# Norms after residual additions taken by pairs of blocks, the root read from PSUM, and the first feed-forward weights split in the mixer

## What is computed

```python
h = rmsnorm(x, norm1_w[l]) * (1.0 + sc1) + sh1      # shifts, scales and gates: silu(c) @ ada_w[l]
x = x + g1 * hybrid_mixer(h, ...)                   # projections, linear attention, SSD, w_out
h = rmsnorm(x, norm2_w[l]) * (1.0 + sc2) + sh2
ff = swiglu(h, ...) if l == 0 else moe_swiglu(h, ...)  # 1024 -> 3584 -> 1024; 8 experts, top 2
x = x + g2 * ff
```

## Time and profile before

| | |
|---|---|
| median of 3 runs | 2882.19 us (2881.25 to 2882.37) |
| profiled execution, its own time | 2881.89 us |
| its span | 2879.9 us, 35798 instructions |
| PE busy | 2536.7 us (88%) |
| DVE busy | 2091.9 us (73%) |
| ACT busy | 1210.8 us (42%) |
| POOL busy | 256.5 us (9%) |
| DMA | 824.78 MB, mean 286 GB/s |

### The profile page before, as it was taken

One profiled execution on the slowest core, in us unless ns is written; L12 is line 12 of the kernel. 1 busy time (PEld: TensorE's weight loads), 2 busy tenths in 40 slices (PEclk: granted clock), 3 DMA queues, 4 the chain that ended last, 5 costly groups with the idle time before them and its releaser, 6 DMA issues. The chain is left out here.

```text
span 2879.9 us, 35798 instructions
## 1 busy us (share of the span) xinstructions
PE 2536.7 (88%) x14026; PEld 2176.6 (76%) x14026; DVE 2091.9 (73%) x2916; ACT 1210.8 (42%) x1310; POOL 256.5 (9%) x280
## 2 busy tenths in 40 slices
PE   4979997986999999999999967997786898887877
PEld 2869996775888888888888855655675888777877
DVE  5758984754988989899899953537736677777764
ACT  2214432214777777777777742103312222222221
POOL 0000000000000000000000000000001334334331
PEclk8988999996999999999999988998998999999899
DMA  7545874443999999999999925211554999999996
GB/s 324 210 171 203 323 278 162 175 187 121 356 356 356 356 357 357 341 351 357 355 356 357 358 93 210 88 58 54 197 218 174 385 403 416 420 421 420 420 421 286
DMA packets 107469, 824.78 MB, mean 286 GB/s; under 512 B 11736, under 2 KB 13912, under 8 KB 14816
## 3 DMA queue, kind: packets, MB, share of 16 engines
q1 hardware_dynamic: 69568, 550.99, 50.1%
q0 software_dynamic: 36864, 268.45, 22.7%
q10 hardware_dynamic: 864, 3.00, 0.3%
HBM read 821.34 MB, written 1.05 MB: 286 GB/s over the span
## 5 line engine op out<-in xcount | busy, mean ns | idle before, releaser
L1537 DVE TENSOR_TENSOR ring_r<-ring,arena_r 128x2048 fp32r<-128x2048 f32 x336 | 770.1, 2292 | 12.2 <-ACT arena_r L1832 0.8
L1832 ACT ACTIVATE arena_r<-ring 128x2048 fp32r<-128x2048 f32 x378 | 725.5, 1919 | 30.9 <-DMA ring<-in_ffn_w_down 14.4
L605 PE MATMUL ps<-arena_r 128*128 128x512 f32 (+1 forms) x1120 | 417.2, 373 | 1.5 <-DVE arena_r L1542 1.5
L607 PE MATMUL ps<-arena_r 128*128 128x512 f32 x896 | 349.3, 390 | 0.0
L606 PE MATMUL ps<-ring_r,arena_r 128*128 128x512 f32 x896 | 348.6, 389 | 0.0
L1181 PE MATMUL ps<-sel,arena 128*128 128x128 f32 x1904 | 252.2, 297 | 76.9 <-ACT sel L1832 76.9
L591 PE MATMUL ps<-h,ring 128*128 128x256 f32 (+2 forms) x1216 | 277.0, 389 | 41.1 <-ACT h L1832 41.1
L1181 PEld LDWEIGHTS ps<-sel,arena 128*128 128x128 f32 x1904 | 245.0, 212 | 84.0 <-ACT sel L1832 83.8
L1181 PE MATMUL ps<-sel,ring 128*128 128x128 f32 x2192 | 265.5, 283 | 37.7 <-ACT sel L1832 37.7
L591 PEld LDWEIGHTS ps<-h,ring 128*128 128x128 f32 (+2 forms) x1216 | 228.1, 189 | 91.7 <-issue 48.0
L1181 PEld LDWEIGHTS ps<-sel,ring 128*128 128x128 f32 x2192 | 259.4, 198 | 42.7 <-ACT sel L1832 42.2
(11 more groups left out here) (244 smaller groups left out, 3614.1 us busy)
## 6 DMA issues: line engine op xcount, KB each, us to landing
ring<-in_moe_w_gate SPq DMA_DIRECT2D x112, 1024.0 KB, 5.7
ring<-in_moe_w_up SPq DMA_DIRECT2D x112, 1024.0 KB, 6.0
ring<-in_moe_w_down SPq DMA_DIRECT2D x112, 1024.0 KB, 5.4
ring<-in_ada_w SPq DMA_DIRECT2D x16, 2048.0 KB, 8.5
ring<-in_w_in SPq DMA_DIRECT2D x10, 2048.0 KB, 10.6
ring<-in_ada_w SPq DMA_DIRECT2D x16, 1024.0 KB, 9.2
ring<-in_w_ada SPq DMA_DIRECT2D x8, 2048.0 KB, 8.1
ring<-in_ffn_w_gate SPq DMA_DIRECT2D x14, 1024.0 KB, 7.1
```

What stands on the lines that cost most here:

```text
L605: e.matmul(out, xs[0], ws[0], start=start, stop=False, skip_group_check=True)
L607: return e.matmul(out, xs[1], ws[0], start=False, stop=stop, skip_group_check=True)
L1537: v(e.tensor_tensor(ring_low[ring.half[unit]], ring.buf[unit], m.high[unit_at[unit] % NHIGH].bitcast(F32), ALU.subtract), ("low", unit))
L1832: A.mark(e.activation(out, src, func, **kw), name)
```

## The change

1. `norm` on ACT squares in four instructions of two blocks, each waiting for its own pair: of the residual additions (norm1 of layer 1, norm2, norm_peer), or of the blocks just scaled (norm_x). PE sums a pair at a time (`norm_sum`). For norm2 the sums stand between the products of the second half of `w_out`, for norm1 of layer 1 in the last `down`, which now runs over output blocks outside and row groups inside and marks each block.
2. `root` on ACT reads the sum from PSUM and makes `sqrt(sum/n + eps)`, with eps from a constant tile that DVE sets at the start; DVE then only takes the reciprocal, after the root. This holds for all norms, `onorm`, `ynorm` and the q, k norms too. The latter get separate root tiles, and the root of context k waits until q has been rotated.
3. `table(func)` makes ACT work on one spare column so that a table is in place: Exp after norm1, Silu at the start of the dense feed-forward, Sqrt at the end of it, of the experts and of the second block.
4. Consumers on PE wait for h block by block (`summed_as`): the low-rank projection, the router, the projections of the second block that have h on the right, and the first query.
5. In the mixer the sum for `ynorm` stands between the two halves of the first `w_out` product; DVE takes 6 pieces (instead of 2) ahead of the reciprocals of `onorm`, and all that are left ahead of `ynorm`'s instead of up to 24 behind the merging.
6. The four first weight halves of the dense feed-forward are taken apart inside mixer 0: on ACT behind `ynorm`'s root, on DVE two ahead of the residuals and one behind each of the first two pairs. The tiles for the high parts are given out in another order.
7. The second load of `cond` into accb in layer 1 moves from ahead of norm2 to behind it. SP loads the first two weights of the second block ahead of the waits for "norm done", the constants and the context.

```diff
+for n in range(2):
+    load(("w_in2", 512 * n), T["w_in2"][n])
...
-for n in range(2):
-    load(("w_in2", 512 * n), T["w_in2"][n])
...
-def norm(name, n=8):
-    b = bank(name)
-    e.wait_ge(*A[name, "squares"])
-    P.mark(summed(b[:, 0:256], [(ones, sq_of[name][:, k, :]) for k in range(n)]), name)
+def norm_sum(name, p, among=HALF):
+    if p == 0:
+        bank(name, among)
+    e.wait_ge(*A[name, "squares", p])
+    for k in (2 * p, 2 * p + 1):
+        last = e.matmul(ps.bank[name][:, 0:256], ones, sq_of[name][:, k, :], start=(k == 0),
+                        stop=(k == 7), skip_group_check=True)
+    if p == 3:
+        P.mark(last, name)
+def norm(name):
+    for p in range(4):
+        norm_sum(name, p, range(8))
+def summed_as(out, pairs, name):
+    for i, (a, b) in enumerate(pairs):
+        e.wait_ge(*A[name, i])
+        last = e.matmul(out, a, b, start=(i == 0), stop=(i == len(pairs) - 1))
+    return last
...
-    b = bank(("ynorm", l), HALF)
-    e.wait_ge(*A["ysq", l])
-    P.mark(summed(b[:, 0:256], [(ones, m.ysq[:, k, :]) for k in range(4)]), ("ynorm", l))
+        if n == 0:
+            b = bank(("ynorm", l), HALF)
+            e.wait_ge(*A["ysq", l])
+            P.mark(summed(b[:, 0:256], [(ones, m.ysq[:, k, :]) for k in range(4)]), ("ynorm", l))
...
+            if mm % 2 and mm > 1:
+                norm_sum(("norm2", l), mm // 2 - 1)
         done(("w_out", l, n))
+    norm_sum(("norm2", l), 3)
...
-    down(6)
+    e.wait_ge(*V["ff low", 6, 3])
+    halves = [[v4(p, 2) for p in split("down", 6, h)] for h in range(2)]
+    for m in range(8):
+        c = slice(128 * m, 128 * m + 128)
+        for j in range(4):
+            high, low = (x[:, j % 2, c] for x in halves[j // 2])
+            last = three(acc(m), (high, low), (fm.acth[0][:, j, :], fm.actl[0][:, j, :]), False, j == 3)
+        P.mark(last, ("ff", m))
+        if m % 2 and m > 1:
+            norm_sum(("norm1", 1), m // 2 - 1)
+    for h in range(2):
+        done(("down", 6, h))
+    norm_sum(("norm1", 1), 3)
...
-    e.wait_ge(*A["hT", "norm2", 1])
     for t in range(2):
-        last = summed(b[:, 8 * t:8 * t + 8],
-                      [(hT[:, k, 128 * t:128 * t + 128], m.rw[:, k, :]) for k in range(8)])
+        last = summed_as(b[:, 8 * t:8 * t + 8],
+                         [(hT[:, k, 128 * t:128 * t + 128], m.rw[:, k, :]) for k in range(8)],
+                         ("hT", "norm2", 1))
...
-        e.wait_ge(*A[ready])
         for j in range(2):
             c = 128 * (2 * (i % 2) + j)
-            last = summed(half(b, j), [(tile[:, k, c:c + 128], rhs[:, k, :]) for k in range(8)])
+            last = summed_as(half(b, j), [(tile[:, k, c:c + 128], rhs[:, k, :]) for k in range(8)], ready)
...
-def rstd(name, src, scale, out):
-    v(e.tensor_scalar(out, src, scale, EPS, ALU.mult, ALU.add))
-    emptied(name)
+def rstd(name, out):
+    e.wait_ge(*A["root", name])
     v(e.reciprocal(out, out), ("rstd", name))
...
-    if name == ("norm2", 0):
-        dense_low("gate", 0, 0)
-    if not first:
-        rstd(name, taken(name)[:, 0:256], 1.0 / D, r)
-    if name == ("norm2", 0):
-        dense_low("up", 0, 0)
-    e.wait_ge(*A["root", name])
     if sc is None:
         v(e.tensor_copy(gs, g))
     else:
         v(e.scalar_tensor_tensor(gs, sc, 1.0, g, ALU.add, ALU.mult))
+    if not first:
+        rstd(name, r)
...
-    some(hidden, 2)
+    some(hidden, 6)
     for p in range(2):
-        b = taken(("onorm", l, p))
-        rstd(("onorm", l, p), v4(b, 2), 1.0 / 128, m.orr[:, 2 * p:2 * p + 2, :])
-    e.wait_ge(*A["root", ("onorm", l, 1)])
...
-    rstd(("ynorm", l), taken(("ynorm", l))[:, 0:256], 1.0 / 512, m.rr1)
-    e.wait_ge(*A["root", ("ynorm", l)])
+    some(hidden, 99)
+    rstd(("ynorm", l), m.rr1)
     for c in range(4):
         v(e.scalar_tensor_tensor(m.merged[:, 4 + c, :], m.yT[:, c, :], pvc(f"ssd_norm_w{l}", c), m.rr1,
                                  ALU.mult, ALU.mult), ("merged", l))
-    some(hidden, 24)
+    if l == 0:
+        dense_low("gate", 0, 0)
+        dense_low("up", 0, 0)
     for i in range(4):
         e.wait_ge(*P["mix", l, 2 * i + 1])
         for mm in (2 * i, 2 * i + 1):
-            residual(acc(mm), mod[l][:, 16:24], mm)
+            residual(acc(mm), mod[l][:, 16:24], mm, ("x", "mix", l, i))
         emptied(("mix", l, i))
-    V.at["x", "mix", l] = V.now
+        if l == 0 and i < 2:
+            dense_low(("gate", "up")[i], 0, 1)
...
-    e.wait_ge(*P["down", 6])
     for m in range(8):
-        residual(acc(m), mod[0][:, 40:48], m)
-    for i in range(4):
-        emptied(("ff", i))
-    V.at["x", "ffn"] = V.now
+        e.wait_ge(*P["ff", m | 1])
+        residual(acc(m), mod[0][:, 40:48], m, ("x", "ffn", m // 2))
+        emptied(("ff", m // 2))
...
-        b = taken(("qknorm", x, p))
-        rstd(("qknorm", x, p), v4(b, 2), 1.0 / 64, m.rr[:, 2 * p:2 * p + 2, :])
-    e.wait_ge(*A["root", ("qknorm", x, 1)])
-    v(e.scalar_tensor_tensor(xx, xx, pvc(g), m.rr, ALU.mult, ALU.mult), ("normed", x))
+        rstd(("qknorm", x, p), m.rr[x][:, 2 * p:2 * p + 2, :])
+    v(e.scalar_tensor_tensor(xx, xx, pvc(g), m.rr[x], ALU.mult, ALU.mult), ("normed", x))
...
-def root(name, out):
-    e.wait_ge(*V["rstd", name])
-    a(out, out, ACT.Sqrt, ("root", name))
-def norm(name, src, sh, dst, scratch, done):
-    a(v4(scratch[:, 0:2048], 8), src, ACT.Square, (name, "squares"))
-    if name == ("norm2", 0):
-        dense_high("gate", 0, 0)
-        dense_high("up", 0, 0)
-    root(name, scratch[:, 2048:2304])
+def root(name, src, n, out):
+    e.wait_ge(*P[name])
+    a(out, src, ACT.Sqrt, ("root", name), scale=1.0 / n, bias=eps)
+    emptied(name)
+def table(func):
+    a(spare, eps, func)
+def norm(name, src, ready, sh, dst, scratch, done):
+    squares = v4(scratch[:, 0:2048], 8)
+    for p in range(4):
+        e.wait_ge(*ready(p))
+        a(squares[:, 2 * p:2 * p + 2, :], src[:, 2 * p:2 * p + 2, :], ACT.Square, (name, "squares", p))
+    root(name, ps.bank[name][:, 0:256], D, scratch[:, 2048:2304])
...
-                a(dst[:, k, :], dst[:, k, :], ACT.Identity, done, bias=sh[:, k:k + 1])
+                a(dst[:, k, :], dst[:, k, :], ACT.Identity, (done, k), bias=sh[:, k:k + 1])
...
-        root(("onorm", l, p), m.orr[:, 2 * p:2 * p + 2, :])
+        root(("onorm", l, p), v4(ps.bank["onorm", l, p], 2), 128, m.orr[:, 2 * p:2 * p + 2, :])
     e.wait_ge(*V["y", l])
     a(m.ysq, m.yT, ACT.Square, ("ysq", l))
-    root(("ynorm", l), m.rr1)
+    root(("ynorm", l), ps.bank["ynorm", l][:, 0:256], 512, m.rr1)
+    if l == 0:
+        for h in range(2):
+            dense_high("gate", 0, h)
+            dense_high("up", 0, h)
...
-    dense_high("gate", 0, 1)
-    dense_high("up", 0, 1)
+    table(ACT.Silu)
...
-    if l == 0:
-        e.wait_ge(*in_x)
-    else:
-        e.wait_ge(*V["x", "ffn"])
-    norm(("norm1", l), xT, mod[l][:, 0:8], hT, scr_end, ("hT", "norm1", l))
+    norm(("norm1", l), xT, lambda p: V["x", "ffn", p] if l else in_x, mod[l][:, 0:8], hT, scr_end,
+         ("hT", "norm1", l))
+    table(ACT.Exp)
     mixer(l)
-    e.wait_ge(*V["x", "mix", l])
+    norm(("norm2", l), xT, lambda p: V["x", "mix", l, p], mod[l][:, 24:32], hT if l else fm.h, scr_end,
+         ("hT", "norm2", l))
     if l:
+        e.wait_ge(*V["x", "mix", l, 3])
         e.dma_start(accb, T["cond"][1]).then_inc(in_c2_again[0], 16)
-    norm(("norm2", l), xT, mod[l][:, 24:32], hT if l else fm.h, scr_end, ("hT", "norm2", l))
...
-e.wait_ge(*V["first done"])
-norm("norm_x", xT, mod[2][:, 0:8], hT, m.scr, "hT x")
+norm("norm_x", xT, lambda p: V["scaled", "final", 2 * p + 1], mod[2][:, 0:8], hT, m.scr, "hT x")
```

More of the change, by code:

```diff
@@ L941, in pe @@
                 P.stage(f"norm{l}")
-                if l:
-                    norm(("norm1", l))
                 mixer(l)
-                norm(("norm2", l))
                 if l == 0:
@@ L1242, in dense_low, with residual @@
                                   fm.high[dense_at[unit] % NHIGH].bitcast(F32), ALU.subtract), ("low", unit))
[L1244 to L1245 removed]
+            def residual(src, gate, m, name=None):
+                v(e.scalar_tensor_tensor(xT[:, m, :], src, gate[:, m:m + 1], xT[:, m, :], ALU.mult, ALU.add), name)
             def ada(t):
@@ L1736, in dve @@
                     for j in range(2):
-                        residual(half(b, j), mod[2][:, 16:24], 4 * n + 2 * p + j)
+                        residual(half(b, j), mod[2][:, 16:24], 4 * n + 2 * p + j, ("x", "second", 2 * n + p))
                     emptied(("mix2", n, p))
-            V.at["x", "second"] = V.now
             m = pr
@@ L1963, in dense_ffn @@
                 dense_high("down", 6, 1)
+                table(ACT.Sqrt)
             def route():
@@ L2157, in act @@
             a(m.filt, m.filt, ACT.Sigmoid, "sigmoid")
+            table(ACT.Sqrt)
             m = pr
             A.stage("peer")
-            e.wait_ge(*V["x", "second"])
```

(2 more changed lines are left out.)

44 lines of the change are left out of this document (23 added, 21 removed).

## The result

The changed kernel takes 2819.78 us (median of 4 runs, 2818.51 to 2821.08), the kernel before 2882.28 in the same comparison: a ratio of 0.9782, 95% interval 0.9771 to 0.9794. That is 62.5 us less; forecast were 69.1 less and 2813, with 2801 to 2830 as the range. The profiled execution has a span of 2816.7 us, 63.2 less than before.

The account below looks back on a forecast made before the run. No engine bounds the whole program; PE or gathers fix the long stretches, so gains come from short norm stretches. Terms 1.9 + 7.2 + 4.3 + 14 + 10.4 + 14 + 5.3 + 12 = 69.1 us off 2882.2: 2813, range 2801 to 2830.

Parts of the forecast that it names:

- output norm, layers 0 and 1, at L784: Linear attention's norm: reciprocals now follow the roots, a loss of 3.2 us in layer 0 and 0.3 in layer 1.
- L784 to first feed-forward product: norm2, layer 0: first feed-forward product 22.6 us after L784 starts, not 33.05; -10.4, or -7.2 with the +3.2 before it.
- dense feed-forward: Layer 0: earlier first activation, less half clock and a shorter stall, -4.3 us in all (2 to 6).
- norm1 of layer 1, from R: From the start R of the last `down`, low-rank product at R + 19.6 us instead of 33.2; -14 after these projections.
- norm2 of layer 1 and routing: Exponential done 37.3 us after L784 starts, before 48.0, with accb landing later: -10.7, with +0.3 -10.4 (4 to 13).
- The stall at 259.91: Dense feed-forward of layer 0: the 4.19 us stall, hanging on the DVE/ACT chain, falls to 2.4 us.
- rival (b): PE returns at 1.2 GHz after every remaining gap and accb loads take longest: 13 us less gain, 2826 us; chance 0.15.
- table** sentence: Each of the four activation table loads taken off the path is worth 1.28 us, not the documented 2.66.
- (c): The clock never falls in the remaining gaps and the dense feed-forward loses its stall: 2802 us; chance 0.10.
- (d): The experts follow a stream that does not shift, so 38 us won before 697 are lost: 2851 us; chance 0.03.
- (e): Some 365 block waits in PE's queue cost 0.28 us each, 102 us in all: 2915 us; chance 0.02.
- table rule (f): A table switch costs 2.66 us with a drain of 1.38, as documented: 2807 us; chance 0.02.

Follow-up runs that it names:

- the experiment: The norms of q, k and context k put back to the old order in the changed kernel: 2824.03 us, ratio 0.98 to the kernel before.
- the first experiment: The changed kernel timed and profiled again, unaltered: 2819.32 us, ratio 0.9779 to the kernel before.
- the run with the early load: The changed kernel with layer 1's load into accb issued ahead of the squares of norm2, not behind the norm: 2819.68 us.
- the first edit alone: The changed kernel with only the norm of the linear attention back in the old order, both layers: 2804.75 us, ratio 0.9722 to the kernel before.

## Why the prediction was right, point by point

| step of the prediction | forecast | measured in the profiles |
|---|---|---|
| start, low-rank product | -2.5 at its start, 1.9 counted | 48.66 to 45.88: -2.8 |
| output norm, layers 0 and 1, at L784 | +3.2, +0.3 | +3.1 against the low-rank product, +0.4 |
| L784 to first feed-forward product | 22.6 us | 205.68 - 182.68 = 23.0 |
| dense feed-forward | -4.3 | -9.7 to -12.2: -2.5 |
| norm1 of layer 1, from R | 19.6 us | 19.8 |
| norm2 of layer 1 and routing | -10.7 | L784 to first expert product 67.8 to 55.3: -12.5 |
| final norm to context norm | -14 | lead 37.9 to 50.7: -12.8 |
| from there to q's sum | 0 | lead 50.7 to 49.0: +1.7 |
| q, k norms | -5.3 | lead 49.0 to 54.1: -5.1 (-5.4 by the experiment) |
| attention, to the last residual pair | 0 | lead 54.1 to 50.8: +3.3 |
| norm_peer | -12 | -12.0 |

The mechanism was right: the long stretches only moved, and the short ones were shortened, norm by norm. The gain is 6.6 us under the forecast of 69.1 by the medians. Mis-sized were these terms. The **dense feed-forward** gave 2.5 instead of 4.3. The stall at 259.91 became this one:

```profile
248.97 0.55 PE L607 MATMUL ps<-h_r,arena_r 128*128 128x256 f32 x1 [3.40 <-DVE ring_r L1266]
```

It is 0.8 us shorter, where 2.4 instead of 4.19 was forecast. Behind it 13 products instead of 28 start at the pace of the low clock (0.21 us from one to the next instead of 0.12), which saves 1.3 of the 2.6 us: the half that I had counted. Ahead of it the first block gained 0.4, not 1.1. The stages **without a term** in the sum, from the context norm to q's sum and the attention, lost 5.0 us of lead (1.7 and 3.3). Both are time at the low clock. For the attention the windows with the first experiment show it, for the rest those of the 36.9 us up to q's sum, the kernel before and the changed one:

```profile
1909.00:1945.90 36.90, 32.20 (x97) 16.81 (x96) 14.39 (x25) 2.25 (x3) 1.19 (x1) 1.00 0.15 57
```
```profile
1860.00:1896.90 36.90, 33.04 (x93) 17.01 (x93) 13.52 (x23) 2.25 (x3) 1.18 (x1) 0.95 0.15 57
```

I had priced the low clock only as rival (b), after the gaps of the norms, not in stages that the change leaves alone. Against that, **routing** gave 1.8 more than forecast. The exponential came 35.6 us after the start of the second half, not 37.3, and the late accb that I charged there costs nothing, which the run with the early load shows. So the total is as near as it is partly by luck: without this gain it would have been 8 us off. The **table** sentence: 1.28 each, as its rows had it.

The prediction took 0.2% as what two runs of this kernel can differ by. The runs of the kernel before beside the experiments go from 2873.27 to 2884.18 us, 0.4%.

One term was right for a reason that I hadn't taken apart. The loss at the output norm was worked out as one chain, with the early sum for `ynorm` in it, and came out at +3.5 as forecast. Its two parts, +14.6 and -11 by the totals, are only seen when each is undone alone.

Rivals (c), (d) and (e) are not seen, nor the table rule (f); (b) in part. What remains open is why the low clock falls where it does: the two profiles of the changed kernel agree, while two programs with the same work in a stage can differ there by 3 us.

## What to carry to other kernels

When a norm stands alone between two long stretches, count what is left after its last input arrives, one pair or one block of each engine's work, and let the consumer start with the first block; here pairs were worth 23 us and the start with the first block 18. Look at each place of a rule by itself: the root ahead of the reciprocal is a gain where the sum comes last, and cost 14.6 us where the reciprocals had lain under another product. And don't take the difference of two profiles at one place for the worth of one edit when two edits meet there.

## What the runs showed of the hardware

A load of the activation table on the path cost its 1.28 us and nothing more. A wait ahead of each of 16 products, 32 instructions, cost PE nothing (7.07 us with and without). The granted clock was the surprise: in 16 us of unchanged work it was 0.71 to 0.74 in four profiles and 1.00 in two, which is 16 of PE's instructions or some 3.5 us. The two profiles of the changed kernel have 0.72 and 0.71 there, so it can be a program's own, and then a median of five runs doesn't remove it. But runs of one program differ by as much, too: those of the first edit alone fall into 2798.81 and 2799.53, and 2804.75 to 2806.20; whether it is this stretch that parts them no profile shows. An edit that is worth under 3 us can be judged in this kernel by the profile, at its place, and hardly by the total.
